# A twenty-first place for experts' weights in a two-block transformer kernel

## The reference

```
h   = rms_norm(x, ffn_norm_g)
g   = argmax(h @ router_group_w)                  # one of 4 groups for each token
two = top_2(softmax(h @ router_expert_w) within g)
for each chosen expert e:                         # 1024 -> 512 -> 1024
    y += gate * (silu(h @ w_gate[e]) * (h @ w_up[e])) @ w_down[e]
x   = x + y
out = rms_norm(x, final_norm_g)
```

## Time and profile before

| | us |
|---|---|
| median of 3 runs | 1683.68 (1682.19 to 1683.75) |
| the profiled execution, its own time | 1686.78 |
| its span, first to last instruction | 1685.1 |
| TensorE matmul busy | 1608.7 (95%) |
| TensorE weight load busy | 1283.4 (76%) |
| VectorE busy | 1003.4 (60%) |
| ScalarE busy | 610.8 (36%) |
| moved by DMA | 415.71 MB, mean 247 GB/s |

### The profile page before, as it was taken

One profiled execution on the slowest core, in us unless ns is written; L12 is line 12 of the kernel. 1 busy time (PEld: TensorE's weight loads), 2 busy tenths in 40 slices (PEclk: granted clock), 3 DMA queues, 4 the chain that ended last, 5 costly groups with the idle time before them and its releaser, 6 DMA issues.

```text
span 1685.1 us, 26100 instructions
## 1 busy us (share of the span) xinstructions
PE 1608.7 (95%) x10490; PEld 1283.4 (76%) x10490; DVE 1003.4 (60%) x1673; ACT 610.8 (36%) x821; POOL 84.5 (5%) x128
## 2 busy tenths in 40 slices
PE   9999999999999999999999999999999988778878
PEld 8999857999998999978899999999964444234333
DVE  7888677788766888876778885797321111111102
ACT  5333346533335333465643344554321000000001
POOL 4000034100000000004200000000000000000000
PEclk9999999999999999999999999999989999999999
DMA  7555452555554555455255555443699999999997
GB/s 297 187 187 187 188 187 76 188 190 188 190 229 175 188 187 187 173 202 188 76 197 192 192 193 203 148 151 125 276 385 420 427 426 428 427 428 427 427 428 299
DMA packets 50396, 415.71 MB, mean 247 GB/s; under 512 B 5744, under 2 KB 5776, under 8 KB 9488
## 3 DMA queue, kind: packets, MB, share of 16 engines
q1 hardware_dynamic: 50256, 414.61, 62.9%
q10 hardware_dynamic: 64, 0.03, 0.0%
HBM read 413.54 MB, written 1.05 MB: 246 GB/s over the span
## 4 chain that ended last, share of the span: by engine, by line
PE 78%; DMA 16%; DVE 3%; ACT 2%; issue 1%; SPq 0%; POOL 0%; POOLq 0%; ACTq 0%; DVEq 0%
PE bank L655 68%; DMA sb_moe_ring<-experts 16%; PE bank L1385 8%; PE bank L852 1%; DMA sb_ring<-weights 0%; DMA sb_h<-xT 0%; DVE sb_ring_lo L2200 0%; ACT sb_high L1680 0%; DVE sb_qk L2703 0%; SPq L561 0%; PE bank L1224 0%; PE bank L943 0%; ACT sb_x_parts L1691 0%; DVE sb_nmax L2361 0%; PE bank L1056 0%
## 5 line engine op out<-in xcount | busy, mean ns | idle before, releaser
L2200 DVE TENSOR_TENSOR sb_ring_lo<-sb_ring,sb_high 128x768 fp32r<-128x768 f32 (+4 forms) x179 | 357.5, 1998 | 120.5 <-ACT sb_high L1680 119.9
L655 PE MATMUL bank<-sb_x_parts,sb_high 128*128 128x512 f32 (+1 forms) x1792 | 404.9, 364 | 1.4 <-DVE sb_ring_lo L2200 1.3
L655 PEld LDWEIGHTS bank<-sb_x_parts,sb_high 128*128 128x128 f32 x1792 | 318.0, 189 | 50.9 <-DVE sb_ring_lo L2200 1.9
L1680 ACT ACTIVATE sb_high<-sb_ring 128x3072 fp32r<-128x3072 f32 x101 | 279.3, 2765 | 105.7 <-PE bank L655 103.5
L655 PE MATMUL bank<-sb_x_parts,sb_ring_lo 128*128 128x256 f32 x1632 | 250.7, 278 | 0.0
L655 PEld LDWEIGHTS bank<-sb_x_parts,sb_ring_lo 128*128 128x128 f32 x1632 | 223.5, 188 | 6.8
L655 PE MATMUL bank<-sb_act_hi,sb_ring_lo 128*128 128x256 f32 x704 | 195.1, 277 | 0.0
L655 PE MATMUL bank<-sb_act_hi,sb_high 128*128 128x256 f32 x672 | 186.2, 277 | 0.0
L655 PE MATMUL bank<-sb_act_lo,sb_high 128*128 128x256 f32 x672 | 185.6, 276 | 0.0
L1723 ACT ACTIVATE sb_expg<-sb_gate_r 128x256 f32<-128x256 f32 x88 | 36.8, 418 | 337.7 <-DVE sb_gate_r L2280 337.7
L1385 PE MATMUL bank<-sb_moe_ring,sb_act 128*32 128x512 f32 x464 | 119.1, 670 | 38.5 <-DMA sb_moe_ring<-experts 38.5
(11 more groups left out here) (461 smaller groups left out, 2135.0 us busy)
## 6 DMA issues: line engine op xcount, KB each, us to landing
sb_ring<-weights SPq DMA_DIRECT2D x133, 1536.0 KB, 6.6
sb_moe_ring<-experts SPq DMA_DIRECT2D x174, 1024.0 KB, 21.6
sb_qk<-experts SPq DMA_DIRECT2D x8, 1024.0 KB, 17.2
sb_front<-experts SPq DMA_DIRECT2D x2, 1024.0 KB, 13.4
sb_oT<-experts SPq DMA_DIRECT2D x2, 1024.0 KB, 16.7
sb_moe_ring<-experts SPq DMA_DIRECT2D x8, 256.0 KB, 17.2
sb_front<-experts SPq DMA_DIRECT2D x2, 768.0 KB, 14.2
sb_h<-xT SPq DMA_DIRECT2D x2, 512.0 KB, 6.5
```

The source lines that it names most:

```text
L655: ins = nc.tensor.matmul(o, l, r, start=start, stop=stop, skip_group_check=True)
L1680: nc.scalar.activation(high_of(n)[:, lo * P:hi * P], ring[:, n % RING, lo * P:hi * P], ACT.Copy).then_inc(done, 1)
L2200: return V.tensor_tensor(ring_lo[:, n % RING, cols], ring[:, n % RING, cols], high_of(n)[:, cols].bitcast(F32), ALU.subtract)
```

## The change

- `MOE_ONCE` goes from 8 to 9: there are 21 places. The new one, 20, is four pieces of 256 KB: the two halves of `rsh`, the other half of `lnv`, and `gate_r`.
- The final norm's weights are no longer in `params` and no longer turned by TensorE and copied by ScalarE. They lie in a row of padding of the dense weights' chunk `mla_in` + 2. One transfer reads that row for all 128 partitions into the place of chunk 180 after that chunk is used; VectorE waits for it (`par_in` 32).
- Places 14 and 11 are loaded first after place 3, and wait for the fourth and the fifth of the state steps (`dn_pe`) instead of `mix_ready` 2. The reading order follows.
- Eight unused products stand where the weights were turned, and three instead of five behind the counts.
- The branch that does not run uses `act` instead of `gate_r`.

```diff
-MOE_ONCE = 8
+MOE_ONCE = 9
-UNUSED_SLOTS = 5
+UNUSED_CHOICE, UNUSED_SLOTS = 8, 3
-IN_PIECES = 19
-MOE_LOADS = [6, 7, 8] + _early + [9, 10, 11, 12, 13, 14, 15] + _late + [16, IN_PIECES]
-MOE_ORDER = [6, 7, 8] + _early + [9, 10, 11] + _late + FREE_PLACES + [12, 13, 14, 15, 16, IN_PIECES]
+IN_PIECES = [19, 20]
+LAST_READ = {14: 4, 11: 5}
+MOE_LOADS = [6, 7, 8] + _early + [14, 11, 9, 10, 12, 13, 15] + _late + [16] + IN_PIECES
+MOE_ORDER = [6, 7, 8] + _early + [11, 9, 10] + _late + FREE_PLACES + [14, 12, 13, 15, 16] + IN_PIECES
...
-        gain_rows = rsh[:, :, :].rearrange("p a t -> p (a t)")
+        gain_rows = moe_ring[:, place_again(MOE_CHUNKS - MOE_RING), 0:D]
...
+                         20: [rsh[:, 0, :], rsh[:, 1, :], lnv[:, 0, :], gate_r[:, :, :].rearrange("p a t -> p (a t)")]}
...
+                elif place in LAST_READ:
+                    sp.wait_ge(dn_pe, LAST_READ[place])
                 elif place < 16:
                     sp.wait_ge(mix_ready, 2)
...
+            sp.wait_ge(moe_free, MOE_CHUNKS - MOE_RING + 1)
+            sp.dma_start(gain_rows, weights[PLAN["mla_in"] + 2][0:1, 2 * D:3 * D].to_broadcast([P, D])).then_inc(par_in, 16)
...
-            for k in range(KD):
-                mm(OUTB[k // 4][:, (k % 4) * P:(k % 4 + 1) * P], col("g_final", k).to_broadcast([P, P]), ident[:], True, True,
-                   turn_h if k == KD - 1 else None)
+            for _ in range(UNUSED_CHOICE):
+                mm(OUTB[0][:, 0:P], ident[:], ident[:], True, True)
...
-            act_e.wait_ge(turn_h, 2)
-            for half in range(2):
-                ins = nc.scalar.activation(gain_rows[:, 512 * half:512 * (half + 1)], OUTB[half][:, :], ACT.Copy)
-            ins.then_inc(h_tok_in, 1)
...
-            dve.wait_ge(h_tok_in, 3)
+            dve.wait_ge(par_in, 32)
```

More of the change, by code:

```diff
@@ L117 @@
           ("fox_qn", 1), ("fox_kn", 1), ("g_mix2", 8), ("conv_a_w", 12), ("conv_a_g", 4), ("dn_conv_w", 48),
-          ("dn_g", 1), ("g_ffn_2", 8), ("g_final", 8), ("inv_freq", 16), ("rope_q", 32), ("rope_k", 32), ("b_f", 16),
+          ("dn_g", 1), ("g_ffn_2", 8), ("inv_freq", 16), ("rope_q", 32), ("rope_k", 32), ("b_f", 16),
           ("a_log", 4), ("dt_bias", 4), ("w_f", 128), ("w_ba", 64), ("w_router", 8 * 36), ("first_wins", 32)]
@@ L397, in moe_place @@
             return front[:, (place - 17) * MCT * P:]
-        expert_pieces = [rstd[:, :, :].rearrange("p a t -> p (a t)"), late_piece[:, :],
-                         grown[:, :, :].rearrange("p a t -> p (a t)"), lnv[:, 1, :]]
+        expert_pieces = {19: [rstd[:, :, :].rearrange("p a t -> p (a t)"), late_piece[:, :],
+                              grown[:, :, :].rearrange("p a t -> p (a t)"), lnv[:, 1, :]],
+                         20: [rsh[:, 0, :], rsh[:, 1, :], lnv[:, 0, :], gate_r[:, :, :].rearrange("p a t -> p (a t)")]}
         def place_parts(place):
-            if place == IN_PIECES:
-                return [(slice(4 * j * P, 4 * (j + 1) * P), piece) for j, piece in enumerate(expert_pieces)]
+            if place in IN_PIECES:
+                return [(slice(4 * j * P, 4 * (j + 1) * P), piece) for j, piece in enumerate(expert_pieces[place])]
             if place == 18:
@@ L420, in two_block_kernel @@
         ring_free = sem("ring_free")
-        moe_in = [sem(f"moe_in{j}") for j in range(IN_PIECES)] + [p_in]
+        moe_in = [sem(f"moe_in{j}") for j in range(IN_PIECES[0])] + [p_in, pos_in]
         moe_free = sem("moe_free")
@@ L1415, in four_tiles @@
                 place, _ = place_of(at + t // MCT)
-                if place == IN_PIECES:
-                    return expert_pieces[t % MCT // 4][:, t % 4 * P:(t % 4 + width) * P]
+                if place in IN_PIECES:
+                    return expert_pieces[place][t % MCT // 4][:, t % 4 * P:(t % 4 + width) * P]
                 if place == 18 and t % MCT >= 12:
@@ L1536, in moe_gathered @@
                 turn_parts(0, 1)
-                pe.wait_ge(h_tok_in, 3)
+                pe.wait_ge(h_tok_in, 2)
                 quad(0, first=True)
@@ L2238, in silu_times_up @@
                 dve.wait_ge(sig_ready, wait_sig)
-                V.tensor_tensor(gate_r[:, b, :], B[b][:, T:2 * T], expg[:, b, :], ALU.mult).then_inc(glu_step, 1)
+                V.tensor_tensor(act[:, b, :], B[b][:, T:2 * T], expg[:, b, :], ALU.mult).then_inc(glu_step, 1)
                 dve.wait_ge(glu_step, reg + (at + 1))
-                V.tensor_tensor(to, gate_r[:, b, :], gate_row, ALU.mult).then_inc(act_ready, 1)
+                V.tensor_tensor(to, act[:, b, :], gate_row, ALU.mult).then_inc(act_ready, 1)
             def x_low_pair(name, i):
@@ L3193 @@
     latents[:KD, :, :QR + KVR + ROPE] = w.reshape(KD, P, -1)
+    latents[KD, 0] = a["final_norm_g_2"]
     mla_in = latents.reshape(3, 3, P, D).transpose(0, 2, 1, 3).reshape(3, P, CT * P)
@@ L3260 @@
         "dn_g": a["dn_norm_g_2"][0][:, None], "g_ffn_2": cols(a["ffn_norm_g_2"][0]),
-        "g_final": cols(a["final_norm_g_2"]),
         "inv_freq": rows(inv),
```

## The result

The changed kernel takes 1689.05 us (1687.45 to 1690.43, 6 runs) against 1682.69 (1681.56 to 1683.75, 6 runs) for the one before: the ratio is 1.0036, 95% interval 1.0027 to 1.0046. It is 6.4 us slower; I had forecast 2.5 us faster.

The account below looks back on a forecast made before the run. The experts' DMA stream of 1 MB chunks, 2.46 us each at 427 GB/s, was taken to bound the end. Terms: -2.46 (place) + 0 + 0.46 (pieces) - 0.47 (products) = -2.47 us, giving 1681.2 us, range 1679.4 to 1684.3.

Parts of the forecast that it names:

- At the kernel's start the parameters lose 8 columns, 4 KB of 389.5: 0: Parameter load at the kernel's start: the shorter transfer was claimed to change nothing, 0 us.
- The filling: Loads before the first refill: chunk 20 joins them in idle DMA time, 4 us spare, one refill fewer, -2.46 us.
- the two early loads: Places 14 and 11, loaded after state steps: end inside the first gap, lengthen the second, worth 0 to 0.5 us, taken 0.
- The unused products: Ahead of the experts, three instead of five behind the counts: gather starts 0.91 us earlier, expert products and first refill -0.47 us.
- rival (c): With fewer unused products the clock stays at 1.2 GHz through gather and first expert products: +3.0 us, 1686.7; chance 0.07.
- The pieces (+0.46): Place 20's four 256 KB parts: first use hidden in the gap, second slows the stream by 0.46 us, bounds 0 and twice that.
- The final norm's weights: Late transfer into chunk 180's place: lands by 1674.0, VectorE needs it at 1676.99, spare 3.0 us, so 0.
- The ring of twelve: Chunk 54 instead of 52 first waits for a reused ring place; 6.6 us to spare, so 0.
- 27 us of work without a DMA wait: Kernel's end: after the last landing TensorE waits for, some 27 us remain, so ending the stream earlier ends the kernel equally earlier.
- (a): Rival: clock rises with the products, pieces cost nothing, loading pauses help: -3.37, up to -4.2 us, about 1680.0; chance 0.17.
- (e): Rival: pieces each pay their own landing, up to +10.3 us on chunk 41, some 1691; chance 0.02.
- (b): Rival: freed places, not bytes, pace the stream; the extra place gives nothing: only -0.47 us, 1683.2; chance 0.14.

Follow-up runs that it names:

- The kernel before with the 32 bytes: The kernel before with an unused buffer of 32 bytes behind params, which moves the buffers behind it up by 32 bytes: 1690.09 us, ratio 1.0037.
- its version with old addresses: The changed kernel plus an unused buffer of 32 bytes behind params, so all SBUF buffers have their addresses of before: 1680.34 us, ratio 0.9982 to before.

## Why the prediction was wrong

The step that failed is two sentences. "At the kernel's start the parameters lose 8 columns, 4 KB of 389.5: 0" priced the transfer and not what the buffer's length does to the addresses behind it. And "1.0486 MB / 427 GB/s = 2.46 us" was carried over to the changed kernel as if the rate could not change, when the runs show it only for rows that start at a multiple of 256 bytes. In the sum it is one missing term: 172 chunks are 180.4 MB, which take 422.1 us at 427.4 GB/s and 429.1 at 420.4 (115.40 and 113.50 MB in 1350 to 1620 us): +7.0 us. The kernel before with the 32 bytes measured +6.9. The changed kernel stands 8.7 above its version with old addresses; 1.7 of that is not placed, and the intervals (some 1.5 us to either side of each) leave room for it.

The other steps, judged by the run at the old addresses (-3.0 us, interval -4.4 to -1.5; forecast -2.47). That the two numbers are close is in part luck, as the first two points show:

- The filling: right in its order. 14 and 11 fill the gap up to 1205, a pause follows near 1227, the place is full before the first refill. But I gave the two early loads "between 0 and 0.5 us, and I take 0", and by the medians the whole gain goes without them. The likely reason is that the first refill comes earlier in other executions than in the one that I read; the medians and the windows fit it, no run separates it. In the changed kernel's trace the second gap is nearly filled to its end (289 GB/s in its emptiest window), which I had named as a sign of being wrong.
- The unused products: the start was wrong, and so, where the clock is high, was "TensorE stays bound by itself". In the changed kernel's trace the six records take 0.91 us, and the gather then waits 0.19 us for the slots (the last row of TensorE above), so not all of what two products less save comes through. Of the -0.47 us the runs can tell nothing: 1.4 us by the medians, within the intervals. I computed with a clock that rises at 1238.80 as if every execution had that. From the last add to h to the gather it is 13.0 us there; in the other traces of kernels with five products 13.0, 11.7, 9.0, 10.1 and 9.0, with three 8.9 to 12.3 (eight traces). So a term of 0.47 us was read out of a stretch that varies by 4 us, and rival (c), a clock that stays low, is no rival but part of the spread.
- The pieces (+0.46): at the old addresses the second uses of places 19 and 20 together cost 0.9 to 1.0 us in two traces (408 and 406 GB/s over 20 us against 427, some 0.46 for each) and 0.4 to 0.5 in three others (417, 418 and 418). That is inside my bounds of 0 and 0.92; the 0.46 itself was read off one execution.
- The final norm's weights: issued at 1663.37, landed 12.2 us later at 1675.6, needed at 1678.40. Spare 2.8 us; I had 3.0.

```profile
L577 SPq DMA_DIRECT2D sb_moe_ring<-weights x1: 434/434/434, 1663.4 to 1663.4; - x1
...
DMA to landing us min/median/max: 12.2/12.2/12.2
...
1678.40 0.69 DVE L3128 TENSOR_TENSOR sb_v_tok<-bank,sb_moe_ring 128x512 f32<-128x512 f32 x1 [2.01 <-ACT sb_sq L2174]
```

- The ring of twelve: DMA share 1.01 throughout. Right.
- The end: the "27 us of work without a DMA wait" belong to that execution. In four of the fourteen traces TensorE waits once more, for the pieces of the last two chunks, by 0.2 to 1.1 us.

Of the rivals none was the cause. (a) to (e) all kept the byte rate of 1 MB chunks fixed; (b) asked what paces the stream and answered with places only. The mark that I had set, a window "between 1247 and 1660 shows less than 420 GB/s", is met by a hair: 419 in one full slice of the page above, 420.4 over the stretch.

## What to carry to other kernels

A term that looks like "the DMA engines' rate" holds for the addresses that it was read at: when an edit changes the length of any buffer, list every DMA destination's start before and after, here by multiples of 256 bytes, before pricing anything else. An unused buffer of 32 bytes was worth 8.7 us. Two parts that each open room for the other (here a place, and the time to fill it) can be worth nothing alone, so judge them together. And a stretch that one execution shows at 1.2 GHz is a sample: read it from several before a term rests on it.

## What the runs showed of the hardware

- Transfers of 8 KB a row from HBM into 128 partitions, queued without a pause: destination rows at a multiple of 256 bytes 427 GB/s (nine traces), 128 or 192 bytes above one 422 (one trace each), 32 or 224 above one 420 (one and two). Other remainders were not run, and why the rate falls is not shown. The Trainium skill, "DMA: Bandwidth & Descriptors", section "How a descriptor splits into AXI transactions", counts beats (of 32 bytes) for transfers that don't start at a multiple of 256 bytes, and finds more of them. It speaks of what is read, and doesn't say whether it holds for the side that is written, which is the side that moved here. The direction agrees; the sizes don't follow that count, by which (an estimate) 32 above would cost 1 beat in 256 and 224 above 7, while the traces have 1.6% for both.
- Matmuls that load fp32 split activations (`x_parts`) and stream split weights (`ring_lo`) took 281 ns instead of 278 each when the two buffers' remainders by 256 bytes were 128 apart (three traces against eleven), and the dense part of this kernel 6 to 8 us more. A shift of both together by 32 bytes did nothing to it (1225.09 after, 1225.11 before).
- TensorE's granted clock on the same instructions differs from execution to execution. Between the last add to h and the gather it was at 1.2 GHz for some 10 us in the trace of before and some 4 us in the changed kernel's; in 14 traces that stretch took 8.9 to 13.0 us.
